# The last 512 of 2048 columns of each modulation piece moved from VectorE to GpSimd

## What is computed

```python
c_act = jax.nn.silu(c)                       # (1, 2048)
mod = c_act @ w_ada[l] + b_ada[l]            # (1, 6 * 2048)
...
modf = c_act @ w_ada_final + b_ada_final     # (1, 2 * 2048)
```

## Time and profile before

| | us |
|---|---|
| median of 3 runs (lowest to highest) | 2416.63 (2412.58 to 2418.13) |
| the profiled execution | 2410.86 |
| its span, first to last instruction | 2409.1 |
| TensorE busy | 2192.5 |
| VectorE busy | 1384.7 |
| ScalarE busy | 724.9 |
| GpSimd busy | 42.9 |

### The profile page before, as it was taken

One profiled execution on the slowest core, in us unless ns is written; L12 is line 12 of the kernel. 1 busy time (PEld: TensorE's weight loads), 2 busy tenths in 40 slices (PEclk: granted clock), 3 DMA queues, 4 the chain that ended last, 5 costly groups with the idle time before them and its releaser, 6 DMA issues. The chain is left out here.

```text
span 2409.1 us, 35878 instructions
## 1 busy us (share of the span) xinstructions
PE 2192.5 (91%) x14533; PEld 1628.1 (68%) x14533; DVE 1384.7 (57%) x2027; ACT 724.9 (30%) x1310; POOL 42.9 (2%) x61
## 2 busy tenths in 40 slices
PE   6999999999999999969999979988888888888886
PEld 5899988788899888868888755444444444444442
DVE  6877788888787888855555544333333333333334
ACT  5443444454444444355554421000000000000001
POOL 0100000000000000030000000000000000000000
PEclk9999999999999999989999989999999999999998
DMA  8877766788777676773434328999999999999996
GB/s 314 325 298 300 272 243 238 305 319 336 302 286 281 244 262 244 296 267 144 163 123 158 140 100 370 430 427 435 427 435 427 434 428 429 431 430 430 431 433 290
DMA packets 71677, 761.73 MB, mean 316 GB/s; under 512 B 8048, under 2 KB 11152, under 8 KB 12560
## 3 DMA queue, kind: packets, MB, share of 16 engines
q1 hardware_dynamic: 71424, 759.45, 78.3%
q10 hardware_dynamic: 144, 0.79, 0.1%
HBM read 757.26 MB, written 2.95 MB: 316 GB/s over the span
## 5 line engine op out<-in xcount | busy, mean ns | idle before, releaser
L2357 PE MATMUL b_ps<-s_raw,s_window 128*64 128x256 f32 x4096 | 455.5, 380 | 84.3 <-DMA s_raw<-in_w_up 43.2
L2357 PEld LDWEIGHTS b_ps<-s_raw,s_window 128*64 128x64 f32 x4096 | 294.3, 137 | 257.0 <-issue 67.0
L1175 DVE TENSOR_TENSOR s_w_tail<-s_raw,s_w_head 128x1024 fp32r<-128x1024 f32 x292 | 344.8, 1222 | 38.9 <-ACT s_w_head L778 38.4
L947 PE MATMUL b_ps<-s_h_head,s_w_head 128*128 128x256 f32 x1184 | 346.0, 292 | 0.0
L948 PE MATMUL b_ps<-s_h_tail,s_w_head 128*128 128x256 f32 x1184 | 338.9, 286 | 0.0
L949 PE MATMUL b_ps<-s_h_head,s_w_tail 128*128 128x256 f32 x1184 | 338.8, 286 | 0.0
L778 ACT ACTIVATE s_w_head<-s_raw 128x1024 fp32r<-128x1024 f32 x292 | 292.7, 1049 | 101.4 <-DMA s_raw<-in_w 74.7
L1262 DVE SCALAR_TENSOR_TENSOR s_ada_acc<-s_raw,s_c_col,s_ada_acc 128x2048 f32<-128x2048 f32 x120 | 282.1, 2351 | 0.0
L2379 PE MATMUL b_ps<-s_down,s_diag 128*64 128x512 f32 x1024 | 226.8, 595 | 15.2 <-ACT s_diag L2308 15.2
L947 PEld LDWEIGHTS b_ps<-s_h_head,s_w_head 128*128 128x128 f32 x1184 | 231.1, 195 | 13.1 <-issue 9.6
L948 PEld LDWEIGHTS b_ps<-s_h_tail,s_w_head 128*128 128x128 f32 x1184 | 231.2, 195 | 0.2
(11 more groups left out here) (344 smaller groups left out, 3000.8 us busy)
## 6 DMA issues: line engine op xcount, KB each, us to landing
s_raw<-in_w SPq DMA_DIRECT2D x198, 1024.0 KB, 5.2
s_raw<-in_w_ada SPq DMA_DIRECT2D x128, 1024.0 KB, 5.3
s_raw<-in_w_gate SPq DMA_DIRECT2D x32, 4096.0 KB, 20.8
s_raw<-in_w_up SPq DMA_DIRECT2D x32, 4096.0 KB, 22.0
s_down<-in_w_down SPq DMA_DIRECT2D x64, 2048.0 KB, 21.8
x_tokens<-in_x SPq DMA_DIRECT2D x1, 2048.0 KB, 7.9
h_t<-in_rel SPq DMA_DIRECT2D x1, 2048.0 KB, 12.1
s_raw<-mod_rows SPq DMA_DIRECT2D x2, 1024.0 KB, 8.9
```

Of the source, the lines that this page charges most:

```text
L947: pe.matmul(out, head, m_head, start=first, stop=False, skip_group_check=True)
L1175: dve.tensor_tensor(w_tail[:, g % SPLITS, cols], raw[:, slot["w", g], cols], w_head[:, g % SPLITS, cols].bitcast(F32), ALU.subtract)\
L2357: ins = pe.matmul(psum[64 * h:64 * h + 64, c // 4, 0:T], window[:, 4 * (c % 4) + k, :], raw[:, c, k * 512 + h * T:k * 512 + h * T + T], st ...
```

## The change

VectorE's modulation step keeps columns 0 to 1535. GpSimd takes columns 1536 to 2047 of every piece: for k = 0 one multiplication into the accumulator; else a multiplication in place in the load's buffer, a wait for it, and an addition to the accumulator. GpSimd now walks through the same list of steps as the other engines; the order of its roots follows from it, and the mask addition comes after modulation piece 24 of the first layer. A new semaphore `ada_last` counts GpSimd's pieces. The load queue waits for it too before it fills a buffer again, and so does TensorE before `ada_sum`.

```diff
--- before.py
+++ after.py
@@ -39,6 +39,7 @@
 SPLITS = 3
 AHEAD = 2
 ADA_PIECES = 64
+ADA_POOL = 1536
 REL_LEN = P + T
 HALF = CHUNK_ELEMS // 2
 LOWEST = -3e38
@@ -488,6 +489,7 @@
                 tally.add("used", i, l)
         for i in range(ADA_PIECES):
             tally.add("ada_done", i, l)
+            tally.add("ada_last", i, l)
     for l, s in flat:
         kind = s[0]
         if kind == "squares":
@@ -716,6 +718,7 @@
                     sp.wait_ge(sem["tail_split"], at("tail_split", (m % n_pieces, 1), m // n_pieces))
                 else:
                     sp.wait_ge(sem["ada_done"], at("ada_done", m % ADA_PIECES, m // ADA_PIECES))
+                    sp.wait_ge(sem["ada_last"], at("ada_last", m % ADA_PIECES, m // ADA_PIECES))
             src = d["w1"] if what == "w" else d["w_ada"]
             sp.dma_start(raw[:, n % RAW, :], src[g]).then_inc(sem[f"raw{n % RAW}"], 16)
             if n == 4 * RAW:
@@ -726,9 +729,8 @@
         pool.memset(half[:, :], -0.5).then_inc(sem["pool_chain"], 1)
         pool.wait_ge(sem["pool_chain"], 1)
         chain = Chain(pool, sem["pool_chain"], 1)
-        for l in range(DEPTH):
-
-
+
+        def x_rstd(l):
             pool.wait_ge(sem["squared"], at("squared", (3, 1), l))
             if l:
                 pool.wait_ge(sem["diag"], at("diag", "low", l - 1))
@@ -738,6 +740,7 @@
             chain.link(pool.tensor_scalar(ssq[:, 0:2], ssq[:, 0:2], 1.0 / D, EPS, ALU.mult, ALU.add))
             pool.tensor_tensor(rstd[:, 0:2], ssq[:, 0:2], half[:, 0:2], ALU.pow).then_inc(sem["rstd"], 1)
 
+        def low_rstd(l):
             for b in (0, 1):
                 for t in range(TT):
                     freed(pool, ("tok", b, t), l)
@@ -748,13 +751,41 @@
                     chain.link(ins)
             pool.tensor_tensor(rstd[:, 2:6], ssq[:, 2:6], half[:, 2:6], ALU.pow).then_inc(sem["rstd"], 1)
 
-            if l:
-                continue
+        def bias_mask():
             pool.wait_ge(sem["consts"], 16 * CONST_LOADS)
             pool.wait_ge(sem["rel_in"], 64)
             for h in range(4):
                 ins = pool.tensor_tensor(c_bias[:, h, :], c_bias[:, h, :], chunk_mask, ALU.add)
             ins.then_inc(sem["bias"], 1)
+
+        last = slice(ADA_POOL, CHUNK_ELEMS)
+        for l, s in flat:
+            if s[0] == "squares" and s[1] == 3 and l < DEPTH:
+                x_rstd(l)
+            elif s[0] == "low_stats":
+                low_rstd(l)
+            elif s[0] == "ada":
+
+                i = s[1]
+                j, k = i // 16, i % 16
+                piece = ("ada", l * ADA_PIECES + i)
+                ring = slot[piece]
+                pool.wait_ge(sem[f"raw{ring}"], at(f"raw{ring}", piece, 0, 16))
+                if k == 0:
+                    if l == 0 and j == 0:
+                        pool.wait_ge(sem["setup_dve"], 5)
+                    if j or l:
+                        full(pool, ("ada_turn", (j - 1) % 4), l if j else l - 1)
+                    ins = pool.tensor_scalar(ada_acc[:, last], raw[:, ring, last], c_col[:, 2, k:k + 1],
+                                             None, ALU.mult)
+                else:
+                    pool.wait_ge(sem["ada_last"], at("ada_last", i - 1, l))
+                    chain.link(pool.tensor_scalar(raw[:, ring, last], raw[:, ring, last], c_col[:, 2, k:k + 1],
+                                                  None, ALU.mult))
+                    ins = pool.tensor_tensor(ada_acc[:, last], ada_acc[:, last], raw[:, ring, last], ALU.add)
+                ins.then_inc(sem["ada_last"], 1)
+                if l == 0 and i == 24:
+                    bias_mask()
 
     @block.scalar
     def _(act):
@@ -1124,6 +1155,7 @@
                 elif kind == "ada_sum":
 
                     pe.wait_ge(sem["ada_done"], at("ada_done", 16 * s[1] + 15, l))
+                    pe.wait_ge(sem["ada_last"], at("ada_last", 16 * s[1] + 15, l))
                     ps = bank_for(pe, s, l)
                     for g in range(4):
                         ins = pe.matmul(ps[32 * g:32 * g + 32, :], ones[:, 0:32], ada_acc[:, 512 * g:512 * g + 512],
@@ -1255,12 +1287,12 @@
                     if k == 0:
                         if j or l:
                             full(dve, ("ada_turn", (j - 1) % 4), l if j else l - 1)
-                        ins = dve.tensor_scalar(ada_acc[:, :], raw[:, ring, :], c_col[:, 2, k:k + 1],
-                                                None, ALU.mult)
+                        ins = dve.tensor_scalar(ada_acc[:, 0:ADA_POOL], raw[:, ring, 0:ADA_POOL],
+                                                c_col[:, 2, k:k + 1], None, ALU.mult)
                     else:
                         dve.wait_ge(sem["ada_done"], at("ada_done", i - 1, l))
-                        ins = dve.scalar_tensor_tensor(out=ada_acc[:, :], in0=raw[:, ring, :],
-                                                       scalar=c_col[:, 2, k:k + 1], in1=ada_acc[:, :],
+                        ins = dve.scalar_tensor_tensor(out=ada_acc[:, 0:ADA_POOL], in0=raw[:, ring, 0:ADA_POOL],
+                                                       scalar=c_col[:, 2, k:k + 1], in1=ada_acc[:, 0:ADA_POOL],
                                                        op0=ALU.mult, op1=ALU.add)
                     ins.then_inc(sem["ada_done"], 1)
                 elif kind == "ada_turn":
```

## The result

The changed kernel takes 2448.62 us, median of 4 runs (2442.90 to 2452.95), against 2416.60 before (4 runs): ratio 1.0137, 95% interval 1.0125 to 1.0149. It is slower by 32 us. The profiled execution took 2452.95 us, the highest of the four, with a span of 2451.1, so the traces differ by 42 us where the medians differ by 32.

A forecast was written before the change was run, and what follows sets the result against it. TensorE (91% busy) was taken as the limit, VectorE second and already the clock in the B heads. Token and output phases 31 us plus heads 20 gave +51: 2462 profiled, 2468 as median, stated as 2465, range 2414 to 2520.

The forecast's parts named there:

- signs of being wrong: Split halves keeping 1.22 us, load-queue waits for GpSimd, or a multiply far from 0.8 us undisturbed would refute the prediction.
- TensorE's waits for the splits: TensorE waiting for VectorE's weight splits: to grow from 5 to tens of us in the profile after.
- Saving on VectorE: Modulation step loses a quarter of its columns: 0.565 us a step, 72 us over 128; worth nothing where TensorE limits.
- Hold of the addition: GpSimd's 512-column add, 1.28 us long, holds up VectorE's next two-SBUF-input instruction for 1.08 us.
- Hold of the multiply: GpSimd's 512-column multiply, taken as 0.8 us long, holds VectorE up 0.6 us (0.47 to 1.08; zero if one-input doesn't disturb).
- Together: Both holds, 1.68 us, less 0.565: +1.12 us a token or output piece on VectorE, 4.53 to 5.65, above TensorE's 5.44.
- Token and output phases: Full hold on every piece, less slack and the split's lead: 7, 18 and 6 us late, 31 us in all.
- Heads: 60% of the hold felt in A and C, 50% in B: A 4, B 2, C 4 us; low-rank 0; twice 10 is 20.
- Waits and queues at no cost: Load queue (buffer work about 4 us) and column sum cost 0; rstd on GpSimd's queue 0, at worst 2 us a layer.
- GpSimd falls behind: Rival, 12%: GpSimd gets turns only after two VectorE instructions; token and output pieces take 6.6 us, about 2500 us.
- Faster, the hold is mostly hidden: Rival, 10%: saving counts fully in B and C heads, about 12 us, 2399 us; needs less than 34% of hold felt.
- No measurable change: Rival, 8%: multiply doesn't disturb VectorE, hold 1.08 us; token and output pieces +0.5, heads +0.1, about 2416 us.

The follow-up runs named there:

- writes_only: Against private, two GpSimd fills of 128x512 that read nothing replace its two instructions; last 512 columns left out: 2396.52 us, ratio 0.9933.
- groups03: Changed kernel with GpSimd's share only in groups 0 and 3 of each layer (token pieces; last three C pieces and output pieces): 2428.23 us, ratio 1.0059.
- groups12: Changed kernel with GpSimd's share only in groups 1 and 2 (A heads; low-rank, B and first seven C pieces): 2438.73 us, ratio 1.0093.
- cols256: Changed kernel with 256 in place of 512 columns on GpSimd, whole result computed: 2426.73 us, ratio 1.0056.
- other_data_wait: As other_data, but the load queue waits for GpSimd before reusing a buffer, as in the changed kernel: 2448.62 us, ratio 1.0153.
- other_data: As private, but GpSimd's second instruction reads two different regions, accumulator and constant table; load queue doesn't wait for GpSimd: 2449.40 us, ratio 1.0148.
- less_alone: Changed kernel without GpSimd's share; VectorE does 1536 columns in 15 of 16 steps, the rest is left out: 2398.77 us, ratio 0.9928.
- mult_only: As private, with GpSimd's multiply of 128x512 alone and without the second instruction: 2405.35 us, ratio 0.9955.
- add_only: As private, with GpSimd's two-input operation of 128x512 alone and without the multiply: 2421.34 us, ratio 1.0021.
- private: Changed kernel with GpSimd's two instructions reading a constant table, not the load's buffer; load queue doesn't wait; last 512 columns left out: 2431.85 us, ratio 1.0059.

## Why the prediction came out as it did

Forecast 2465 us, range 2414 to 2520, slower 82%; measured 2448.62. The mechanism was right and is now shown by experiment: GpSimd's reads hold VectorE up, for longer than the columns that were taken from it had cost. The forecast sum of 51 us was 19 too high. One of the prediction's signs of being wrong came true (the multiply takes 1.56 us undisturbed, far from 0.8), and TensorE's waits for the splits, forecast to grow to tens of us, fell. So the loss reaches TensorE by another path than the one that was summed up. By its own steps:

*Saving on VectorE*, 0.565 us a step: a free step of 1536 columns takes 1.81 us in the median, 0.54 below 2.35. Right. What it is worth alone, 12 us in the rival's sum, is 16.

*Hold of the addition*, 1.08 us: 1.07. Right, and scaled rightly from the 128x256 additions of the mask. The reading "its own length less 0.2" held at three sizes or forms (1.07 of 1.26, 0.85 of 1.04, 0.49 of 0.73).

*Hold of the multiply*, 0.6 us: 0.41. The instruction is twice as long as I took it (1.56 against 0.8) and holds less, so the rule that gave 0.6 from 0.8 is wrong for it.

The Trainium skill's rule in "SBUF — State Buffer", section "Who interferes with whom", that the loser is blocked for the whole instruction, fits the addition nearly and the multiply not at all (0.41 of 1.56). The other rule of that section of the Trainium skill, that a GpSimd instruction that only writes doesn't contend with a two-input one on VectorE, is what "writes_only" shows. The 769 ns that the Trainium skill gives in "GPSIMD Engine Reference", section 3.1, for a tight loop over 512 elements is half of the 1561 ns measured for this operation. The prediction said that by the rule of the whole instruction its sum would be some 20 us higher; that counts 0.20 us once a piece, and there are two instructions, so by its own scheme it would have been some 38.

*Together*, 1.68 us a piece: 1.07 + 0.41 = 1.48 where both holds fall in full, and a token piece of 5.48 us on VectorE and not 5.65. But the sum took the full hold for each of the 58 pieces in token and output phases, and that is the step that was mis-sized. From the means of the two VectorE groups in those phases, the split halves and the modulation steps are held for 0.92 us a piece: the rest of GpSimd's time falls where VectorE does something else or waits, or GpSimd is the one that waits. With 0.54 saved, a piece is 0.4 us longer in the mean and not 1.12, some 4.9 us, below TensorE's 5.44. Token and output phases, forecast 31 us, lost 11 in the trace and 13 in "groups03".

*Heads*, forecast 20 us, lost 26 in the trace and 23 in "groups12"; C was forecast 4 a layer and lost 6 and 3; low-rank with B was forecast 2 and lost 7 and 7. The hold of the two groups is smaller there than forecast too, 0.64 us a piece in the mean against 0.8 to 1.0, so the size of the hold isn't what makes them lose more. One cause is in the B heads, against the earlier trace rows:

```profile
310.28 0.52 DVE L1372 TENSOR_SCALAR s_s_buf<-s_s_buf,s_stat 128x128 f32<-128x128 f32 x1
...
310.99 3.42 DVE L1207 TENSOR_TENSOR s_w_tail<-s_raw,s_w_head 128x1024 fp32r<-128x1024 f32 x2
...
320.41 3.44 DVE L1207 TENSOR_TENSOR s_w_tail<-s_raw,s_w_head 128x1024 fp32r<-128x1024 f32 x2
```

A piece now takes 9.42 us in place of 8.97 (forecast +0.28, found +0.45). The row at 310.28 is a scaling of the probabilities with one input in SBUF, which I had let pass for free. Over the block, the group of this form and that of a PSUM-input one, first before, then after:

```profile
L1241 DVE TENSOR_TENSOR s_gate_raw<-b_ps,s_rrow 128x256 f32<-128x256 f32 x32 | 13.4, 419 | 0.0
...
L1340 DVE TENSOR_SCALAR s_s_buf<-s_s_buf,s_stat 128x128 f32<-128x128 f32 x24 | 6.9, 286 | 0.8
```

```profile
L1273 DVE TENSOR_TENSOR s_gate_raw<-b_ps,s_rrow 128x256 f32<-128x256 f32 x32 | 13.3, 417 | 0.0
L1372 DVE TENSOR_SCALAR s_s_buf<-s_s_buf,s_stat 128x128 f32<-128x128 f32 x24 | 11.0, 457 | 0.8
```

The one-input operation in SBUF went from 286 to 457 ns, the one from PSUM stayed (419 and 417). In "SBUF — State Buffer", section "Who interferes with whom", the Trainium skill names `tensor_scalar` among the operations that can contend; I had not applied it. These operations stand between softmax and TensorE's transpose, which waits for them (line 1136). Over the block VectorE's busy time grew by 56 us; the split halves and the modulation steps account for 34, so some 20 us lie in such small instructions. How much of the heads' loss is theirs isn't measured apart.

*The clock* was no term of the sum, and half of the trace's loss stands with it. That the stalls bring the dips is argued from rows such as those above, not shown: "cols256" has 39 us of idle time in the block, 9 more than before, and the same 14 us of clock not granted, and in the kernel before some dips follow windows of 4 us with only 0.56 us of idle time (a clock of 0.57 from 730 to 734 us), while others follow 3 us of it.

*Waits and queues at no cost*: right for the load queue ("other_data_wait"), though GpSimd had a buffer's work in hand for 5.0 us (129.34 to 134.30) and not 4. The column sum's wait grew by 5.5 us, for VectorE and not for GpSimd. The rstd wait (line 1309) grew from 4.1 to 9.1 us, a little over the bound of 4 more.

*The rivals.* "GpSimd falls behind": its premise came true for the multiply, which gets its turn only after two VectorE instructions, but not for the addition. The load queue waits for GpSimd 23 times, 29.8 us in all, and the pair "other_data" and "other_data_wait" shows that such waits cost nothing. "Faster, the hold is mostly hidden" asked for less than 34% felt, on the plain rule that a felt microsecond is a lost one. The experiments give a better scale: the hold per piece where it falls in full, VectorE's busy time by the profile's pages over that of less_alone (1324.4), and the time over less_alone.

| kernel | full hold, us a piece | VectorE busy over less_alone, us | time over less_alone, us |
|---|---|---|---|
| less_alone, writes_only | 0 | 0, -1 | 0, -2 |
| mult_only | 0.42 | 24 | 7 |
| before (0.565 of own work in its place) | none | 60 | 16 |
| add_only | 0.85 | 68 | 23 |
| private | 1.27 | 92 | 33 |
| other_data | 1.48 | 116 | 51 |

(The last row and writes_only were measured beside other runs of the kernel before, which differ by 0.2 us.) The busy time holds what really was held, small instructions included: 116 us over 128 pieces is 0.91 a piece and not 1.48. By interpolation between mult_only and add_only the time crosses that of the kernel before at a full hold of about 0.68 us, an estimate; the trade sits at 1.48. The last column follows VectorE's busy time nearly, whether a hold or its own work fills it, and the price rises: 28% of the first 24 us are lost, 44% of all 116. That fits slack which is used up first, but no run shows that reason. The step from private to other_data alone is 24 us more busy time and 18 us of time. The trade took VectorE from 60 to 116 us on this scale, and so the kernel from 16 to about 50.

"No measurable change" asked for a multiply that doesn't disturb; "add_only" is that case, with a shorter second instruction, and gives 1.0021, about there.

No kernel here that computes the whole result with a share on GpSimd beats the kernel before. Those that beat it leave the 512 columns out. What stays open is by which path the loss reaches TensorE in the A heads, where it looked like the limit: by small instructions that come late, or by the lower clock. No run tells these apart.

## What to carry to other kernels

Before work is moved from VectorE to GpSimd, look in the trace for a stretch where both are active, and read VectorE's duration there against its usual one: that difference per column, not GpSimd's own time, is the price. Here a column on GpSimd cost VectorE 2.9 ns where the holds fell in full (1.48 us / 512), 1.8 ns in the mean (0.91 / 512), and had cost 1.1 ns at home; neither 512 nor 256 columns paid. Then ask how often the two meet: a forecast that takes every meeting in full is too high, as this one was. And look at more than the engine's total: VectorE was 80% busy in the first block (798 of 993 us) beside a limiting TensorE, and its small operations on the softmax path were late all the same.

## Not expected of the hardware

- A GpSimd multiply by a per-partition scalar, 128x512, takes 1.56 us, more than the two-input addition's 1.26.
- It holds a pair of split halves up for 0.41 us only, and is itself in hand for 3.59 us beside them, up to 7.38 elsewhere.
- A two-input GpSimd instruction that reads one region twice takes 1.04 us in place of 1.26, and holds 0.85 in place of 1.07.
- Fills on GpSimd (0.53 us for 128x512) hold nothing up.
